# Two transformer blocks on one core: where the low halves of weights and norms are made, fp16 lookups in the routing, and four moves of small steps

## The chip, the core and the metric

One core of one Trainium2 chip runs the whole program in one launch. The metric is the device time of one execution in microseconds. TensorE is the matrix engine, VectorE (DVE) and ScalarE (ACT) the elementwise engines, GpSimd (POOL) the fourth, and SyncE (SP) issues most transfers.

## What is computed

The input is x, 256 tokens by 1024, in float32. The first block is modulated by a condition vector. It has two attentions (a sparse one with an index score and top 64 keys, and a "stick-breaking" one with cumulative products), and then a product-key mixture of experts: each token takes 16 of 128 sub-keys on two sides, 16 of their 256 sums, and so 16 of 16384 experts for each of 8 heads. The second block has a mixer (short convolution, block attention, gated linear attention), a cross attention on a memory of 256 tokens, and a convolutional ffn of width 2752. Cut to what the change touches, the routing of the experts is

```
s1, i1 = lax.top_k(s[:, :, 0], PEER_TOPK)
s2, i2 = lax.top_k(s[:, :, 1], PEER_TOPK)
cand = (s1[..., :, None] + s2[..., None, :]).reshape(t, PEER_HEADS, PEER_TOPK * PEER_TOPK)
cand_idx = (i1[..., :, None] * N_KEYS + i2[..., None, :]).reshape(t, PEER_HEADS, PEER_TOPK * PEER_TOPK)
top_s, pos = lax.top_k(cand, PEER_TOPK)
eidx = jnp.take_along_axis(cand_idx, pos, axis=-1)
```

## The kernel before

**Split products.** Every float32 product is made of three products of rounded halves: high by high, high by low, low by high. Weights stream in units of 128 x 1024. For each unit ScalarE casts the high half (`splits`, L1334, with the cast in L1343), and VectorE (`lows_until`, L1888, L1894) or POOL (`units`, L2696, L2702) subtracts it from the unit to get the low half. TensorE waits in `unit` for the low of a unit (semaphore `lo_v` or `lo_g`) and makes 24 matmuls with it, in the ffn and the projections 24 of 256 columns, in v 12 of 512 (all through the helper in L635). SyncE loads the next unit into a slot once the low of the slot's last unit is there.

**The order of work.** A plan (`stream_plan`) lists all units: w_ada, the projections of the first block up to w_o, then w_pq (16 units, queries of the routing), u (128), v (128), the w2 units, w_up (43) and w_dn (22). `lead_of` (L241) says how many units ahead of TensorE a high half is cast, `buffers` (L110 and below) gives from it, for each position i, the units whose cast (`hi_at[i]`) and whose low (`lo_at[i]`, one position later and never behind the unit) are made there. `on_pool` (L250) says which lows POOL makes: every second one in w_pq and in u before unit 56 (TB0), every third from u 120 to the ffn and in the ffn, with some left out, among them w2_o to w2_xo. Each engine runs its own program over the same list. Steps that are not weights (attention, routing, norms) are generators in `Jobs`; at each unit an engine takes one step of up to three of them, so that `yield` spaces them by units.

**Routing** (`route_steps`, L2264, on VectorE, one step a unit from w_pq on). Eight passes of three steps find the 16 best of 128 key scores (MAX8, FIND_INDEX8, MATCH_REPLACE8, L2281 to L2295); eight times three steps make and search the 256 candidates of a head (L2309 to L2326); then, for two halves of the tokens, some small operations (L2340 to L2351) and two lookups. A lookup turns 128 positions (8 heads x 16) into indices: it compares them with 0 to 15 (L2359, 2048 elements), multiplies with the 16 indices (L2362, 2048) and sums over the 16 (L2367). All in float32. TensorE transposes the results beside u 45 and u 52, and from u 54 on the gates are placed.

**Norms.** VectorE scales a tile (L1980), ScalarE rounds it to the high half, and POOL makes the low half (`norm_steps`, L2723, L2729) for norm 2 (the memory, beside v), norm 3 (in front of the mixer) and norm 5 (in front of the ffn). Norm 1, which has a shift, has its low on VectorE (L1984).

**Behind w_o.** The first two units of w_pq multiply the unscaled rows. VectorE then scales their results (L2254 to L2259) and ScalarE copies them out with a bias (L1635) when `q_r` says so; its cast of w_pq 4 comes after that.

**Stick masks.** POOL masks the diagonals of the stick attention (L2779, L2784) in two rounds of four heads, and adds the index mask to the position bias of eight heads (`masked`, L2766), six of them between the halves of the first round and behind it.

**Gated linear attention** (`gla_steps`: L1192 TensorE, L1763 ScalarE, L2516 VectorE, L2812 POOL). It starts behind w2_mv and the block attention; its first steps make the decays (L1770 to L1785: Abs, Exp, Ln, then the exponentials of their sums).

Of the kernel before, what the change touches and what calls it, by code (L numbers as in the profile page):

```python
# [210 lines left out]
def stream_plan():  # L211
# [29 lines left out]
    def lead_of(i):  # L241
        return 0 if i < QI0 - 1 else 4 if QA0 - 2 <= i < PA0 else 3 if i < PQ0 + 1 else 2 if i < XK0 - 2 else 3 if i < XL0 else 4 if i < XL0 + 2 else 5 if i < UP0 else 6
# [87 lines left out]
def scaled_before(q):  # L330

    return q - (q > 4)
# [38 lines left out]
def build(nc, A, out, scratch, x_kept):  # L371
    with ExitStack() as ctx:
# [98 lines left out]
        eq = PR[:, o96 + 6144:o96 + 8192]  # L471
        qh = [PR[:, 22528 + i * 512:22528 + (i + 1) * 512] for i in range(3)]
# [7 lines left out]
        tb = [z.bitcast(F16) for z in (flat(rT[:, 0:4, :]), xTf[:, 0:1024], xTf[:, 1024:2048])]  # L480
        t_row = [z[:, 0:512].rearrange("p (a i b) -> p a i b", a=2, b=2) for z in tb]
# [64 lines left out]
        mg_sum, mg_hi, mg_lo, pk_mm, pk_s = (sem(n) for n in ("mg_sum", "mg_hi", "mg_lo", "pk_mm", "pk_s"))  # L546
        rt_c, rt_d, rt_e, rt_f, rt_p, rt_m = (sem(n) for n in ("rt_c", "rt_d", "rt_e", "rt_f", "rt_p", "rt_m"))
# [81 lines left out]
        def tensor_program(t):  # L629
# [552 lines left out]
            lin("w2_mk", 4, hk, mh, both=True, alone=4)  # L1182
            one("w2_lr", hk, mh)
            lin_nat("w2_mv", hkt, mh, 512)

            def need_m():
                t.wait_ge(*evac("w2_mq", 1))
                t.wait_ge(*evac("w2_mk", 1))

            jobs.start(attend(ATT_M, need_m, lambda: t.wait_ge(*evac("w2_mv", 1))))  # L1190

            def gla_steps():  # L1192
# [3 lines left out]
                St = bmm[:, 2048:2816].rearrange("p (c e) -> p c e", c=3)  # L1196
                o = claim(6)
# [16 lines left out]
                yield  # L1214
                yield
                yield
# [42 lines left out]

            jobs.start(gla_steps())  # L1260
            lin("w2_gk", 2, hk, mh)
# [68 lines left out]
        def scalar_program(s):  # L1330
# [310 lines left out]

            def gate_weights(tt):
                s.wait_ge(rt_d, tt + 1)
                S.activation(g2[:, tt, :], g2[:, tt, :], ACT.Exp).then_inc(rt_e, 1)
# [115 lines left out]
            nat_copy("w2_mv", mv, 512)  # L1760
            jobs.start(attend(ATT_M, lambda: None))

            def gla_steps():  # L1763
# [4 lines left out]
                dec = sm[:, 120:124]  # L1768
                s.wait_ge(g_p, 1)
# [16 lines left out]
                yield  # L1786
                yield
                yield
# [22 lines left out]
            jobs.start(gla_steps())  # L1811
            lin_copy("w2_gk", 2, gqk)
# [71 lines left out]
        def vector_program(v):  # L1884
# [90 lines left out]
            def norm_steps(i, src, gain, shift=None):  # L1975
                for j in range(8 if shift is None else 10):
# [5 lines left out]
                    if shift is not None and j >= 2:  # L1982
                        v.wait_ge(n_hi, 8 * scaled_before(i) + j - 1)
                        V.scalar_tensor_tensor(out=H[:, 1, j - 2, :], in0=rT[:, ROW[(j - 2) % 4], :], scalar=shift(j - 2),  # L1984
# [268 lines left out]
            norm(1, xT, lambda j: sm[:, 24 + j:25 + j], shift=lambda j: mod[:, 24 + j:25 + j])  # L2253
            V.tensor_copy(rT[:, 1, :], recip(1)).then_inc(q_r, 1)  # L2254
# [9 lines left out]
            def route_steps():  # L2264
# [69 lines left out]
                e3, e4 = eq.rearrange("p (a i) -> p a i", i=16), eq.rearrange("p (h k i) -> p h k i", h=8, k=16)  # L2334
                io = iota[:, 0:16].rearrange("p (o i) -> p o i", o=1).broadcast_to((128, 128, 16))
# [683 lines left out]
```

## Time and profile before

| | |
|---|---|
| median of 3 runs | 1407.16 us (1403.23 to 1407.29) |
| the profiled execution's own time | 1406.49 us |
| its span, first to last instruction | 1404.8 us |
| mean granted clock of TensorE | 0.993 |
| busy: TensorE, VectorE, ScalarE, POOL | 97%, 77%, 60%, 25% |
| chain that ended last: TensorE, VectorE, ScalarE | 78%, 14%, 4% |

All durations below are of the one profiled execution. A row of the timeline gives the start from the first instruction of the span, the time to the end of the last instruction merged in it, engine, line, operation, what it writes and reads, and in brackets how long the engine was idle before it and whose work ended that. Matmuls are pipelined and their ends are modelled, so the spacing of starts is read rather than the busy share.

### The profile page before, as it was taken

How to read it: one execution, taken by the hardware profiler on the slowest of the kernel's cores; microseconds unless marked ns; L12 is line 12 of the kernel's file. 1: busy time of each engine (PE TensorE's matmuls, PEld its weight loads, DVE VectorE, ACT ScalarE, POOL GpSimd, SP SyncE). 2: the span in 40 equal slices, each digit the busy share in tenths (PEclk: the TensorE clock that was granted, in tenths of full speed). 3: DMA queues.
4: the chain of work that ended last, by engine and by line, in shares of the span. 5: the costliest groups of instructions: out<-in, count | busy, mean ns of one | idle time of the engine just before them, and what ended most of it. 6: DMA issues, size and time to landing. Idle time of an engine off the chain costs nothing.

```text
span 1404.8 us, 25319 instructions
## 1 busy us (share of the span) xinstructions
PE 1363.8 (97%) x10144; PEld 1265.8 (90%) x10144; DVE 1082.1 (77%) x1857; ACT 836.9 (60%) x1457; POOL 354.2 (25%) x223
## 2 busy tenths in 40 slices
PE   7999999999998999999999999999999999999997
PEld 5988989999998999999988888887888889899997
DVE  7789898668899888899576666677667577898862
ACT  3556776454553688787554444565556667777641
POOL 3216101234444000000222322343222221343200
PEclk9999999999999999999999999999999999999998
DMA  9859775556664555555566666666666536376630
GB/s 385 278 193 304 238 246 173 196 166 191 194 185 150 166 163 157 162 153 163 167 224 192 195 190 195 222 189 185 193 208 250 184 103 187 106 237 203 205 107 31
DMA packets 73719, 268.21 MB, mean 191 GB/s; under 512 B 8401, under 2 KB 9730, under 8 KB 72834
## 3 DMA queue, kind: packets, MB, share of 16 engines
q1 hardware_dynamic: 71280, 256.41, 57.9%
q10 hardware_dynamic: 1426, 7.56, 1.5%
q0 software_dynamic: 896, 2.62, 0.5%
q8 instruction: 81, 1.33, 0.4%
q14 instruction: 36, 0.29, 0.1%
HBM read 262.88 MB, written 3.67 MB: 190 GB/s over the span
## 4 chain that ended last, share of the span: by engine, by line
PE 78%; DVE 14%; ACT 4%; DMA 1%; issue 1%; POOL 0%; DVEq 0%; ACTq 0%; POOLq 0%
PE bank L635 78%; DVE split L1894 4%; DVE ada_acc L1929 2%; DVE PR L2362 1%; ACT split L1343 1%; DMA ringb<-in_w_ada 1%; DVE PR L2359 1%; DVE rT L1980 1%; DVE PR L2367 0%; PE bank L816 0%; DMA ringb<-in_w_g 0%; ACT PB L1460 0%; DVE H L2448 0%; DMA vecs<-in_vecs 0%; DVE MH L1996 0%
## 5 line engine op out<-in xcount | busy, mean ns | idle before, releaser
L635 PE MATMUL bank<-H,split 128*128 128x256 f32 x5832 | 704.6, 281 | 14.1 <-DVE split L1894 12.9
L635 PEld LDWEIGHTS bank<-H,split 128*128 128x128 f32 x5832 | 682.8, 189 | 20.6 <-DVE split L1894 15.9
L1343 ACT CAST split<-ringb 128x1024 fp32r<-128x1024 f32 x350 | 365.6, 1047 | 270.5 <-PE bank L635 254.7
L635 PE MATMUL bank<-split,H 128*128 128x512 f32 (+1 forms) x1728 | 390.1, 387 | 1.5 <-ACT PB L1362 1.4
L635 PEld LDWEIGHTS bank<-split,H 128*128 128x128 f32 x1728 | 320.4, 188 | 69.1 <-issue 1.8
L2702 POOL TENSOR_TENSOR split<-ringb,split 128x1024 fp32r<-128x1024 f32 x88 | 218.5, 2484 | 640.5 <-ACT split L1343 640.5
L1894 DVE TENSOR_TENSOR split<-ringb,split 128x1024 fp32r<-128x1024 f32 x262 | 332.1, 1271 | 58.9 <-ACT split L1343 58.8
L2448 DVE TENSOR_TENSOR H<-PR,H 128x256 fp32r<-128x256 f32 x128 | 135.1, 1056 | 105.5 <-ACT H L1697 105.4
L1894 DVE TENSOR_TENSOR split<-far,split 128x1024 fp32r<-128x1024 f32 x78 | 102.5, 1322 | 32.1 <-ACT split L1343 31.9
L1343 ACT CAST split<-far 128x1024 fp32r<-128x1024 f32 x89 | 92.7, 1048 | 53.0 <-PE bank L635 40.0
L2716 POOL TENSOR_TENSOR rT<-rT 128x256 f32<-128x256 f32 x25 | 28.9, 1156 | 174.5 <-ACT rT L1392 172.9
L1673 ACT ACTIVATE PR<-bank 128x512 f32<-128x512 f32 (+31 forms) x59 | 28.6, 485 | 61.8 <-PE bank L635 61.1
L635 PE MATMUL bank<-act_t,split 128*128 128x256 f32 x528 | 60.3, 276 | 0.1
L635 PEld LDWEIGHTS bank<-act_t,split 128*128 128x128 f32 x528 | 60.0, 188 | 0.3 <-DVE act_t L2671 0.3
L1655 ACT ACTIVATE xT<-cst,rT 128x128 f16<-128x128 f32 x168 | 55.2, 435 | 0.0
L2421 DVE SCALAR_TENSOR_TENSOR PR<-bank,PR 128x224 f32<-128x224 f32 (+31 forms) x64 | 33.3, 520 | 27.6 <-PE bank L635 27.1
L1697 ACT CAST H<-PR 128x256 fp32r<-128x256 f32 x128 | 51.1, 400 | 0.5 <-PE bank L635 0.5
L635 PE MATMUL bank<-Ym,split 128*128 128x256 f32 x336 | 41.5, 283 | 1.5 <-DVE Ym L2055 1.5
L635 PEld LDWEIGHTS bank<-Ym,split 128*128 128x128 f32 x336 | 40.2, 189 | 2.1 <-DVE split L1894 1.7
L2702 POOL TENSOR_TENSOR split<-far,split 128x1024 fp32r<-128x1024 f32 x11 | 28.2, 2562 | 53.9 <-ACT split L1343 53.9
L635 PE MATMUL bank<-PA 64*128 64x256 f32 (+4 forms) x176 | 25.9, 372 | 8.3 <-POOL PA L2739 8.3
L1929 DVE SCALAR_TENSOR_TENSOR ada_acc<-ringb,cond,ada_acc 128x1024 f32<-128x1024 f32 x24 | 32.2, 1343 | 1.5 <-DMA ringb<-in_w_ada 0.8
(307 smaller groups left out, 1266.2 us busy)
## 6 DMA issues: line engine op xcount, KB each, us to landing
ringb<-in_u SPq DMA_DIRECT2D x128, 512.0 KB, 3.9
ringb<-in_v SPq DMA_DIRECT2D x128, 512.0 KB, 4.5
ringb<-in_w_ada SPq DMA_DIRECT2D x28, 512.0 KB, 5.8
far<-in_w_up SPq DMA_DIRECT2D x26, 512.0 KB, 4.7
far<-in_w_ada SPq DMA_DIRECT2D x20, 512.0 KB, 5.3
ringb<-in_w_up SPq DMA_DIRECT2D x17, 512.0 KB, 4.7
ringb<-in_w_pq SPq DMA_DIRECT2D x16, 512.0 KB, 4.0
far<-in_w_dn SPq DMA_DIRECT2D x14, 512.0 KB, 3.8
```

The costliest lines, as they stand in the source:

```text
L635: return TE.matmul(o, l, r, start=start, stop=stop, skip_group_check=True)
L1343: S.copy(buf(m)[0], slots[P.slot[m]]).then_inc(hi_done, 1)
L1655: S.activation(z[:, i // 2, :, i % 2], iota, ACT.Abs, bias=cpn[:, 4 * g + i:4 * g + i + 1]).then_inc(t_abs, 1)
L1673: ins = S.activation(d[:, :, n:T], o[:, :, n:T], ACT.Gelu)
L1697: S.copy(cf[i % 8][0], P3[:, i, :]).then_inc(c_hi, 1)
L1894: V.tensor_tensor(lo, slots[P.slot[m]], hi.bitcast(F32), ALU.subtract).then_inc(lo_v, 1)
L1929: V.scalar_tensor_tensor(out=acc, in0=w, scalar=cond[:, k:k + 1], in1=acc, op0=ALU.mult, op1=ALU.add).then_inc(ada_done, 1)
L1980: V.scalar_tensor_tensor(out=rT[:, ROW[j % 4], :], in0=src[:, j, :], scalar=gain(j), in1=recip(i), op0=ALU.mult, op1=ALU.mult).then_inc(n_ ...
L2421: V.scalar_tensor_tensor(out=d[:, 0:n, :], in0=o[:, 0:n, :], scalar=DOWN16, in1=d[:, 0:n, :], op0=ALU.mult, op1=ALU.mult).then_inc(t_out, 1)
L2448: V.tensor_tensor(lo, P3[:, i, :], hi.bitcast(F32), ALU.subtract).then_inc(c_lo, 1)
L2702: G.tensor_tensor(lo, slots[P.slot[m]], hi.bitcast(F32), ALU.subtract).then_inc(lo_g, 1)
L2716: G.tensor_tensor(acc, acc if k > 1 else rT[:, square_row(q, 0), :], rT[:, square_row(q, k), :], ALU.add).then_inc(sq_add, 1)
```

## The change

1. `on_pool`: outside the ffn and the first two units of w_qi POOL makes no weight low any more; VectorE makes them. The lows of norms 2, 3 and 5 move to VectorE's `norm_steps`, one for each tile, two tiles behind the scaling. POOL's `norm_steps` goes.
2. The lookups run on fp16 in another order of axes: positions and indices are cast, compared with a table of 0 to 15 that ScalarE writes once (`io16`), multiplied, and summed by three additions that halve the length (2048, 1024, 512) and a last one that writes float32.
3. `lead_of` is 3 up to w_pq 2, so that ScalarE casts w_pq 4 in front of the copy of the first queries; VectorE calls `unit` and `lows_ahead` once in front of its copies, and later for five units instead of six.
4. POOL adds the index mask of heads 2 to 7 (twelve additions) in one piece behind the first round, instead of in two pieces.
5. The generator of the gated linear attention starts in front of w2_mv and of the attention; one `yield` comes first, and three yields behind the decays become six.

```
     def lead_of(i):
-        return 0 if i < QI0 - 1 else 4 if QA0 - 2 <= i < PA0 else 3 if i < PQ0 + 1 else 2 if i < XK0 - 2 else ...
+        return 0 if i < QI0 - 1 else 4 if QA0 - 2 <= i < PA0 else 3 if i < PQ0 + 3 else 2 if i < XK0 - 2 else ...
...
-        if XK0 - 1 <= i < XK0 + 7:
-            return False
-        return (PQ0 <= i < U0 + TB0 and i % 2 == 0) or (i >= U0 + TB0 + 64 and i % 3 == 0)
+        return i >= UP0 and i % 3 == 0
...
+            s.wait_ge(n_lo, 8 * scaled_before(1) + 8)
+            S.copy(io16.rearrange("p (i q) -> p i q", i=16), iota[:, 0:16]...broadcast_to((128, 16, 128))).then_inc(rt_i, 1)
...
             def norm_steps(i, src, gain, shift=None):
-                for j in range(8 if shift is None else 10):
+                both = MH if i == 2 else H
+                for j in range(10):
...
-                    if shift is not None and j >= 2:
+                    if j >= 2:
                         v.wait_ge(n_hi, 8 * scaled_before(i) + j - 1)
+                    if j >= 2 and shift is None:
+                        V.tensor_tensor(both[:, 1, j - 2, :], rT[:, ROW[(j - 2) % 4], :], both[:, 0, j - 2, :].bitcast(F32), ALU.subtract).then_inc(n_lo, 1)
...
+            unit("w_pq")
+            lows_ahead()
             V.tensor_copy(rT[:, 1, :], recip(1)).then_inc(q_r, 1)
...
+                v.wait_ge(rt_i, 1)
+                behind(0)
+                for tt in range(2):
+                    rc.up(V.tensor_copy(tf16[:, tt, :, :, :], tf[:, tt, :, :].rearrange("p (h c) i -> p c i h", c=2)))
...
-                        rc.up(V.tensor_tensor(e3, io, ps_, ALU.is_equal))
+                        rc.up(V.tensor_copy(pos16.rearrange("p (k h) -> p k h", k=16), pos))
+                        behind(0)
+                        rc.up(V.tensor_tensor(tri3(e16, 16), tri3(io16, 16), pos16...broadcast_to((128, 16, 128)), ALU.is_equal))
                         yield
                         behind(0)
-                        rc.up(V.tensor_tensor(e4, e4, tk, ALU.mult))
+                        rc.up(V.tensor_tensor(by(e16, 16), by(e16, 16), tk, ALU.mult))
                         yield
...
+                        for dst, src in ((e8, e16), (e4_, e8), (e2, e4_)):
+                            n = dst.shape[1]
+                            behind(0)
+                            rc.up(V.tensor_tensor(dst, src[:, 0:n], src[:, n:2 * n], ALU.add))
                         behind(0)
-                        V.tensor_reduce(cpf[:, tt, s2, :], e3, AX, ALU.add).then_inc(rt_f, 1)
+                        V.tensor_tensor(pos, e2[:, 0:128]..., e2[:, 128:256]..., ALU.add).then_inc(rt_f, 1)
...
-            units("w_pq", 6)
+            units("w_pq", 5)
...
-                if w == 0:
-                    masked(range(2, 5))
                 for i in range(4):
                     g.wait_ge(k_e2, 4 * w + i + 1)
                     G.tensor_tensor(diagonals(zs[i][1]), diagonals(zs[i][1]), up2, ALU.mult).then_inc(k_m2, 1)
                 if w == 0:
-                    masked(range(5, 8))
+                    masked(range(2, 8))
...
-            units(8)
-            jobs.start(norm_steps(2))
-            units(39)
+            units(8 + 39)
             jobs.finish()
             units(2 + 1)
+            g.wait_ge(c_lo, 128)
             G.memset(uv[:, :, 0:2], 0.0).then_inc(cv_z, 1)
...
-            norm(3)
...
-            norm(5)
```

On TensorE, ScalarE and VectorE alike the fifth item reads (TensorE's shown):

```
+            lin("w2_mk", 4, hk, mh, both=True, alone=4)
+            one("w2_lr", hk, mh)
             jobs.start(gla_steps())
+            lin_nat("w2_mv", hkt, mh, 512)
...
+            jobs.start(attend(ATT_M, need_m, lambda: t.wait_ge(*evac("w2_mv", 1))))
```

## Rows read from the trace of the kernel before

**Rows 1.** The page, busy time of each engine (share of the span) and instructions.

```profile
PE 1363.8 (97%) x10144; PEld 1265.8 (90%) x10144; DVE 1082.1 (77%) x1857; ACT 836.9 (60%) x1457; POOL 354.2 (25%) x223
```

**Rows 2.** Who TensorE waited for: us in total, times, longest us.

```profile
PE bank L635 <- DVE split L1894: 12.9, 9, 2.5
```

**Rows 3.** Busy us of each engine by stretch, granted clock, transfer share, GB/s.

```profile
319.14:335.46 16.32, 16.32 (x146) 16.32 (x146) 13.07 (x68) 7.75 (x9) 7.21 (x3) 1.00 0.66 195
351.78:368.10 16.32, 16.32 (x146) 16.32 (x146) 14.27 (x40) 7.76 (x9) 7.22 (x3) 1.00 0.67 196
...
413.18:461.87 48.69, 41.95 (x331) 41.15 (x330) 48.48 (x28) 20.52 (x24) 20.43 (x7) 0.93 0.49 149
```

**Rows 4.** Timeline of TensorE from 400 to 480: start, us, instructions merged.

```profile
423.24 13.23 PE L635 MATMUL bank<-H,split 128*128 128x256 f32 x96 [2.35 <-DVE split L1894]
...
436.55 11.55 PE L635 MATMUL bank<-H,split 128*128 128x256 f32 x96
450.30 5.71 PE L635 MATMUL bank<-H,split 128*128 128x256 f32 x48 [2.19 <-DVE split L1894]
458.14 4.62 PE L635 MATMUL bank<-H,split 128*128 128x256 f32 x24 [2.13 <-DVE split L1894]
...
462.85 11.14 PE L635 MATMUL bank<-H,split 128*128 128x256 f32 x96
```

**Rows 5.** Timeline of VectorE from 405 to 463.

```profile
415.50 4.38 DVE L2362 TENSOR_TENSOR PR<-PR 128x2048 f32<-128x2048 f32 x1
419.80 3.38 DVE L1894 TENSOR_TENSOR split<-ringb,split 128x1024 fp32r<-128x1024 f32 x1
```

**Rows 6.** Groups of VectorE instructions over the whole span: busy us, mean ns, idle.

```profile
L2309 DVE TENSOR_TENSOR PR<-PR 128x256 f32<-128x256 f32 x16 | 11.9, 784 | 0.1
...
L2359 DVE TENSOR_TENSOR PR<-cst,PR 128x2048 f32<-128x2048 f32 x4 | 9.2, 2288 | 0.1
L2665 DVE TENSOR_TENSOR ftmp<-ftmp 128x256 f32<-128x256 f32 x22 | 9.1, 415 | 0.0
```

**Rows 7.** Groups of VectorE from 500 to 650, where POOL does nothing.

```profile
L1894 DVE TENSOR_TENSOR split<-ringb,split 128x1024 fp32r<-128x1024 f32 x46 | 56.0, 1218 | 0.0
...
L2399 DVE TENSOR_TENSOR rt<-rt,cpw 128x512 f16<-128x512 f16 x45 | 18.7, 416 | 0.0
```

**Rows 8.** Timeline of POOL.

```profile
419.67 2.43 POOL L2702 TENSOR_TENSOR split<-ringb,split 128x1024 fp32r<-128x1024 f32 x1 [1.94 <-ACT split L1343]
```

**Rows 9.** Timeline around the fifth unit of w_pq, all engines, then TensorE alone.

```profile
258.71 0.51 ACT L1436 ACTIVATE H<-rT,mod 128x256 fp32r<-128x256 f32 x1 [0.28 <-DVE rT L1980]
...
261.16 0.84 ACT L1635 ACTIVATE PR<-bank,sm 128x256 f32<-128x256 f32 x2 [1.95 <-DVE bank L2259]
261.89 1.99 ACT L1343 CAST split<-ringb 128x1024 fp32r<-128x1024 f32 x2
...
264.25 4.58 PE L635 MATMUL bank<-H,split 128*128 128x256 f32 x24 [2.54 <-DVE split L1894]
```

**Rows 10.** Timeline of POOL and of TensorE around the norm of the memory.

```profile
936.01 2.38 POOL L2702 TENSOR_TENSOR split<-ringb,split 128x1024 fp32r<-128x1024 f32 x1 [4.88 <-ACT split L1343]
...
971.02 2.39 POOL L2702 TENSOR_TENSOR split<-ringb,split 128x1024 fp32r<-128x1024 f32 x1 [5.71 <-ACT split L1343]
...
937.35 1.46 PE L635 MATMUL bank<-rT,cst 128*128 128x256 f32 x6
```

**Rows 11.** Timeline of TensorE from 1076 to 1128.

```profile
1078.20 9.49 PE L635 MATMUL bank<-H,split 128*128 128x256 f32 x72
1089.00 5.73 PE L635 MATMUL bank<-H,split 128*128 128x256 f32 x48 [1.31 <-DVE split L1894]
...
1116.16 3.07 PE L635 MATMUL bank<-split,H 128*128 128x256 f32 x24 [1.36 <-ACT PB L1362]
...
1123.62 1.30 PE L635 MATMUL bank<-PB 64*128 64x128 f32 x16 [0.90 <-ACT PB L1472]
```

**Rows 12.** Timeline of TensorE in the stage of the stick attention.

```profile
128.90 1.46 PE L635 MATMUL bank<-zbuf,PA 128*64 128x256 f32 x8 [1.12 <-POOL zbuf L2784]
```

More of the change, by code:

```diff
@@ L241, in lead_of @@
     def lead_of(i):
[L242 removed]
+        return 0 if i < QI0 - 1 else 4 if QA0 - 2 <= i < PA0 else 3 if i < PQ0 + 3 else 2 if i < XK0 - 2 else 3 if i < XL0 else 4 if i < XL0 + 2 else 5 if i < UP0 else 6
     P.buffers(ring_of, lead_of, {QI0 + 2: QI0 + 1}, (7,))
@@ L471, in build @@
         eq = PR[:, o96 + 6144:o96 + 8192]
+        eq16 = eq.bitcast(F16)
+        e16, e8, e4_, e2, pos16 = (eq16[:, a:b] for a, b in ((0, 2048), (2048, 3072), (3072, 3584), (3584, 3840), (3840, 3968)))
+        tf16 = cand.bitcast(F16).rearrange("p (t c i h) -> p t c i h", t=2, c=2, i=16)
         qh = [PR[:, 22528 + i * 512:22528 + (i + 1) * 512] for i in range(3)]
@@ L1181, in tensor_program @@
             mh = normed(3)
[L1182 to L1190, printed above, removed]
             def gla_steps():
@@ L1213, in gla_steps @@
                 last.then_inc(g_p, 1)
-                yield
-                yield
-                yield
+                for _ in range(6):
+                    yield
                 t.wait_ge(g_v, GV["qk"])
@@ L1640, in scalar_program @@
                     jobs.start(key_scores(i))
+            s.wait_ge(n_lo, 8 * scaled_before(1) + 8)
+            S.copy(io16.rearrange("p (i q) -> p i q", i=16), iota[:, 0:16].rearrange("p (i q) -> p i q", q=1).broadcast_to((128, 16, 128))).then_inc(rt_i, 1)
             def gate_weights(tt):
@@ L1785, in gla_steps @@
                 S.activation(dec, bT[:, 63:256:64], ACT.Exp).then_inc(g_a, 1)
-                yield
-                yield
-                yield
+                for _ in range(6):
+                    yield
                 for i in range(2):
@@ L1811, in scalar_program @@
             jobs.start(gla_steps())
+            nat_copy("w2_mv", mv, 512)
+            jobs.start(attend(ATT_M, lambda: None))
             lin_copy("w2_gk", 2, gqk)
@@ L2512, in vector_program @@
             unit("w2_lr")
-            units("w2_mv", 4)
-            jobs.start(attend(ATT_M, lambda: v.wait_ge(bmm_in, 16)))
             def gla_steps():
@@ L2531, in gla_steps @@
                 V.tensor_scalar(la, la, 1.0 / 16.0, None, ALU.mult).then_inc(g_v, 1)
-                yield
-                yield
-                yield
+                for _ in range(6):
+                    yield
                 v.wait_ge(g_a, GA["dec"])
@@ L2576, in vector_program @@
             jobs.start(gla_steps())
+            units("w2_mv", 4)
+            jobs.start(attend(ATT_M, lambda: v.wait_ge(bmm_in, 16)))
             units("w2_gk", 2)
@@ L2721, in adds @@
                     pass
-            def norm_steps(i):
-                for j in range(8):
-                    tmp = rT[:, ROW[j % 4], :]
-                    both = MH if i == 2 else H
-                    hi, lo = both[:, 0, j, :].bitcast(F32), both[:, 1, j, :]
-                    g.wait_ge(n_hi, 8 * scaled_before(i) + j + 1)
-                    G.tensor_tensor(lo, tmp, hi, ALU.subtract).then_inc(n_lo, 1)
-                    yield
-            def norm(*a, **k):
-                for _ in norm_steps(*a, **k):
-                    pass
             g.wait_ge(rb_in, 16)
```

22 lines of the change are left out of this document (16 added, 6 removed).

## The prediction

> **What bounds the kernel.** I read the page first: TensorE is busy for 97% of the span [rows 1], so time can only come from its idle gaps, from matmuls that run slowly, or from less work. The change takes no matmul away. The view of who waited for whom gives TensorE 12.9 us behind the weight lows of VectorE, the largest wait after the start [rows 2]. The timeline of TensorE then says where. A unit of weights is 24 matmuls of 256 columns and takes 2.72 us when nothing is late: six units last 16.32 us, of which POOL makes three lows [rows 3]. In the lookups of the routing, behind 413 us, there are gaps of 2.35, 2.19 and 2.13 us, all ended by a low [rows 4]. Two of the batches behind them are also slow: 13.23 us for 96 matmuls against 11.14 for the same 96 at 462.85, and 4.62 us for 24, where 24 matmuls end after 2.99 (5.71 for 48, less 2.72). The granted clock of that stretch is 0.93 [rows 3]: part of it ran at 1.2 GHz instead of 2.4. With 0.4 us in the batch at 436.55 (11.55 against 11.14), the stretch loses 6.67+2.09+1.63+0.4 = 10.8 us.
>
> Why are those lows late? Three things must be seen together. The product of a lookup, 2.29 us when alone, took 4.38, and the low behind it 3.38 instead of 1.22 [rows 5 to 7]. At 419.80 that low began 0.13 us after POOL's own low of 2.43 us [rows 8], and took nearly the sum of the two. In the stretch 413.18 to 461.87 VectorE is busy 48.48 of 48.69 us [rows 3]. Its work there is four lookups of three operations on 2048 elements, 2.29 us each (27.5), seven lows (8.5) and some 1.6 us of small ones, 37.6 us in all. So about 11 us are VectorE standing behind POOL, since both read two SBUF tensors.
>
> The Trainium skill says the same in "GPSIMD Engine Reference", Key points: the SBUF interfaces are shared, and VectorE contends when it has two SBUF inputs. The trace agrees with its 3.38 us.
>
> **The change, part by part.** The sum is made against the profiled execution, 1406.49 us (span 1404.8); the median of the three runs is 0.67 higher.
>
> (a) Lookups. The 36 to 37 lows that POOL makes in w_pq and u before unit 56 go to VectorE, and each lookup becomes a chain of seven fp16 operations. A tensor_tensor of 512 fp16 took 416 ns, one of 256 fp32 415 ns, one of 2048 fp32 2288 ns [rows 6, 7]; so 148 ns plus 1.045 ns for each pair of halves. 2048 halves then take 1.22 us, 1024 0.68, 512 0.42, 256 0.28; the cast of positions and the last sum (128 elements of fp32) 0.28 each. A lookup is 0.28+1.22+1.22+0.68+0.42+0.28+0.28 = 4.38 us. Bounds: 4.38 from these rows, and 7.5 if every form makes one element per step only (0.28+2.29+2.29+1.22+0.68+0.42+0.28). I take 4.38, since the rows of 512 have a broadcast operand too. The stretch holds 14 units (331 matmuls), 38.1 us at full speed. VectorE needs 17.5 for lookups, 14 lows of 1.22 (17.1), 1.6 of small ones and up to 0.8 for the two copies of the index table: 37.0 us. It fits. I leave 0.5 us for a step that is late: the stretch gives back **10.3 us** (about 3 at the 7.5 bound).
>
> The Trainium skill, "VectorE: DVE Perf Modes", What auto-detection actually checks, wants every tensor in 16 bits with step one for the doubled rate; its table gives 1224 ns for 2048. By it comparison, product and the first three sums qualify, and the cast and the last sum do not.
>
> What pays for the lows elsewhere? In the search of the key scores six units show 13.07 us of VectorE work [rows 3]. Three more lows of 1.22 make 16.7 against 16.32: 0.4 us late in six units, 0.9 in the thirteen such units behind w_pq (in w_pq the key-score matmuls leave more room). In the candidate stage it is 14.27+3.66, less what its four sums at L2309 no longer lose to POOL (784 ns on average instead of 415, 1.5 in all [rows 6]), so 16.4: just what there is. A low is made a unit ahead: its cast can start two units (5.44 us) before TensorE needs it and takes 1.0 (two in 1.99 [rows 9]), the low 1.22, which leaves a reserve of 3 us. The cover is this reserve; if it is used up, each further unit costs 0.1 us. ScalarE's new copy of the position table (2048 elements, about 2 us by its casts of 1024) stands in front of one cast and eats 2 of the 3 us once. Cost: nothing.
>
> The same skill page, The DRAIN you can't avoid, lets no operation start before the pipe of the last is empty. By it lows take their full 1.22 us, as counted above; with the overlap that neighbouring starts show the stretch needs 1.1 us less.
>
> (b) Fifth unit. TensorE waits 2.54 us for the low of w_pq 4 and then needs 4.58 us for 24 matmuls instead of 2.99: 4.1 us. The cast stands on ScalarE behind two ACTIVATEs of 0.84 us, which wait 1.95 us for VectorE [rows 9]. With a lead of 3 it comes before that wait, when the norm's last activation ends at 259.2, and ends at 260.2. On VectorE the new call that would make the low stands before the copies only by its name: the plan puts low 4 at the position of w_pq 2, and unit and lows_ahead reach w_pq 1 alone. So the low follows the copies, which release ScalarE at 261.16, and ends near 262.4; TensorE was free 2.54 us before 264.25, at 261.7. 0.7 us remain, and without the long gap I expect no fall of the clock: **3.4 us**.
>
> (c) Norm of the memory. POOL's weight lows come every 8.16 us; from 936.01 to 971.02 the distance is 35.01 instead of 32.64, and six summing matmuls explain some 1.2 of the 2.37 between [rows 10]. **1.1 us** come from the loop scale, two casts, coefficient low, weight low, in which POOL holds VectorE up by 0.34 a unit. On VectorE the norm's low lies under the casts.
>
> (d) Norm 3. 72 matmuls from 1078.20 and the gap to 1089.00 take 10.80 us, 8.16 at full speed: 2.6 lost, 1.31 of it behind a low [rows 11]. Now VectorE waits for the cast at every tile (added wait: behind it are the weight lows, and TensorE behind these), and its lows 2 and 3 come after take_queries and a weight low: I work out 1.7 us of waits. **0.9 us** gained (0 to 2.3). Norm 5 is hidden by the unscaled units: nothing.
>
> (e) Decay steps. They issue no DMA; those that they need are issued before. Their three activations with table loads move from the attention to w2_mv, where ScalarE has one cast per unit and a lead of three units. The waits of 1.36 and 0.90 us for ScalarE's copies [rows 11] go: **2.25 us** (0 to 2.3). Next late would be the softmax chain.
>
> (f) Stick masks. The 1.12 us wait for POOL's mask [rows 12] ends with ScalarE's exponential, not with POOL's queue. What can be gained is VectorE's delay by six mask additions; they return later in one block of twelve. Between +1.5 and -1, I take **0.4 us**. The c_lo wait before the memset has only two sums behind it, and these wait for later work.
>
> Lows in u's end and in v (40) cost nothing: VectorE has room, and slots come free earlier. Sum: 10.3+3.4+1.1+0.9+2.25+0.4 = 18.4 us; 1406.5-18.4 = **1388.1 us**.
>
> **Rivals.** (1) VectorE is full. For: the search stage needs 16.7 of 16.32. Against: the lookups have room, and the reserve covers 0.1 us a unit for thirty units. If fp16 forms run at one element per step, VectorE needs 49.5 us where 38.1 and a reserve of 3 are there; and TensorE loses some 8 us again; 18.4-8 = 10.4 are left: 1396. Chance 0.14. (2) Slower: POOL is not what lengthens VectorE's instructions; transfers or ScalarE are, in the whole route stage. Then all 65 lows of the stage can take 2.2 us instead of 1.22 (64 us on top), and one in two of them 32; less 3 us of reserve and about 6 of room in w_pq some 23 are left, and the time is 1388+23 = 1411. It decides from 3.1 us of VectorE work per unit. Against: without POOL 46 lows average 1218 ns [rows 7]. 0.03. (3) The fifth unit's edit does not do what it says beyond the lead, and the clock still falls there: 1390 to 1392. 0.05. (4) More is freed than counted, in the stick stage and the mixer: 1383. 0.10. (5) The moves of (c) to (f) cancel and the lookups give half: 1403. 0.05. Forecast: 0.63.
>
> **Numbers.** A measurement of this kernel tells 0.3% (4.2 us) from no change. Cases 1, 3, 4 and the forecast are faster, 0.92; case 5 counts as same; case 2 as slower. The range 1382 to 1397 takes in all but 2 and 5.
>
> **What would show it.** Right: no gap over 1 us and a clock of 1.00 between 405 and 463 us, fp16 comparisons of 1.22 us, no VectorE low over 1.5 us before the ffn, a gap near 0.7 us in front of w_pq 4, none at w2_gk. Wrong: comparisons near 2.3 us, new gaps in the candidate stage, or lows of 2 us and more with POOL idle.

## The result: 1391.9 us after 1405.3, and the profile after

The changed kernel takes 1391.91 us, median of 11 runs (1387.92 to 1400.02); the kernel before takes 1405.30 beside it (1401.45 to 1411.5, 11 runs). The ratio is 0.9907, 95% interval 0.9891 to 0.9923. 13.4 us are gone where 18.4 were forecast. Every ratio leaves out runs at a clearly lower granted clock, such as one of 1689.55 us at 0.753 among the repeats of the changed kernel. The profiled execution took 1391.84 us (span 1390.0, 14.8 less than before).

Who TensorE waited for, after (us in total, times, longest):

```profile
PE bank L638 <- DVE split L1900: 3.8, 7, 0.8
...
PE bank L638 <- DVE H L1992: 1.5, 1, 1.5
...
PE bank L638 <- POOL zbuf L2792: 0.6, 1, 0.6
```

The 12.9 us of [rows 2] are 3.8, and the longest wait for a weight low is 0.8 instead of 2.5. New is L1992, the norm lows on VectorE. Busy time by stretch (us, then PE, PEld, DVE, ACT, POOL, granted clock, transfer share, GB/s):

```profile
409.10:452.10 43.00, 43.00 (x368) 43.00 (x367) 38.18 (x61) 22.42 (x26) 0.00 (x0) 1.00 0.59 185
318.67:335.62 16.95, 16.95 (x146) 16.95 (x145) 16.37 (x71) 7.75 (x9) 0.00 (x0) 1.00 0.60 194
```

Both stretches answer to [rows 3]. The one with the lookups has TensorE busy throughout and a clock of 1.00 where it was 0.93. But look at the second row: 146 matmuls, six units of weights, take 16.95 us instead of 16.32, with TensorE busy all the time, no wait, and a granted clock of 1.00. The groups of VectorE from 403 to 452 show the lookups (busy us, mean ns):

```profile
L1900 DVE TENSOR_TENSOR split<-ringb,split 128x1024 fp32r<-128x1024 f32 x18 | 22.0, 1221 | 4.6 <-ACT split L1346 4.3
L2378 DVE TENSOR_TENSOR PR<-rT,PR 128x2048 f16<-128x2048 f16 x4 | 4.9, 1226 | 0.1
L2381 DVE TENSOR_TENSOR PR<-PR 128x2048 f16<-128x2048 f16 x4 | 4.9, 1219 | 0.0
L2388 DVE TENSOR_TENSOR PR<-PR 128x1024 f16<-128x1024 f16 x4 | 2.7, 685 | 0.0
L2388 DVE TENSOR_TENSOR PR<-PR 128x512 f16<-128x512 f16 x4 | 1.7, 425 | 0.1
L2390 DVE TENSOR_TENSOR PR<-PR 128x128 f32<-128x128 f16 x4 | 1.6, 389 | 0.1
L2388 DVE TENSOR_TENSOR PR<-PR 128x256 f16<-128x256 f16 x4 | 1.2, 292 | 0.1
L2376 DVE CAST PR<-PR 128x128 f16<-128x128 f32 x4 | 1.1, 264 | 0.0
```

An fp16 comparison takes 1226 ns where the fp32 one took 2288 [rows 6], a low 1221 where one took 3.38 us [rows 5]. The timeline of TensorE, after:

```profile
261.18 3.00 PE L638 MATMUL bank<-H,split 128*128 128x256 f32 x24 [0.44 <-DVE split L1900]
...
304.44 127.45 PE L638 MATMUL bank<-H,split 128*128 128x256 f32 x1080
...
1068.51 13.60 PE L638 MATMUL bank<-H,split 128*128 128x256 f32 x114 [1.51 <-DVE H L1992]
...
1211.84 0.62 PE L638 MATMUL bank<-H,split 128*128 128x256 f32 x3 [0.51 <-DVE split L1900]
1212.97 12.30 PE L638 MATMUL bank<-H,split 128*128 128x256 f32 x106 [0.51 <-DVE split L1900]
```

The wait in front of w_pq 4 is 0.44 us instead of 2.54 [rows 9], and the granted clock stayed at 1.00 behind it. 1068.51 is norm 3, and 1211.84 and 1212.97 are two waits in front of the scaled units of w_up, where before had none. The waits of 1.36 and 0.90 us in the mixer [rows 11] are gone.

**Where the time went.** Both kernels issue the same 8856 matmuls on weights, so the start of the nth can be compared. By stretch, the distance between two such starts, before and after, in us:

| stretch | before | after | difference |
|---|---|---|---|
| to the first matmul, and up to the stick stage (600 matmuls) | 130.28 | 128.53 | -1.75 |
| fifth unit (1440 to 1488) | 11.54 | 7.98 | -3.56 |
| u, units 5 to 37 (1872 to 2664) | 89.76 | 93.28 | +3.52 |
| lookups, u from unit 38 (2664 to 3024) | 53.00 | 42.99 | -10.01 |
| norm of the memory (5860 to 6100) | 55.45 | 54.40 | -1.05 |
| norm 3, w2_mq and w2_mk (6480 to 6552) | 10.80 | 10.35 | -0.45 |
| mixer (6552 to 6888) | 65.99 | 63.13 | -2.86 |
| start of the scaled w_up (7380 to 7500) | 13.99 | 15.19 | +1.20 |
| all other stretches | | | +0.2 |

The third line is the surprise: 792 matmuls, no gap among them in either kernel, and 3.52 us more. Row 304.44 above holds them.

**Two paces.** In every trace of this study a matmul of 256 columns starts either 113.3 or 117.7 ns behind the last, for hundreds of matmuls on end, at a granted clock of 1.00. The group view of TensorE from 325 to 400 us shows it in the mean (busy us, mean ns), first before, then after:

```profile
L635 PE MATMUL bank<-H,split 128*128 128x256 f32 x665 | 75.5, 276 | 0.0
```

```profile
L638 PE MATMUL bank<-H,split 128*128 128x256 f32 x639 | 75.4, 281 | 0.0
```

665 against 639 matmuls in the same 75 us. Between two such weight matmuls that follow each other directly, I add up what the distance of their starts is over 113.3 ns. Where that is under 20 ns it is called slow pace here: 10.0 us in the trace of before and 14.4 in that of after. What is over 20 ns is called late starts, and matmuls at the low clock, each some 100 ns over, are in it too: it falls from 37.5 to 23.2 us. So the late starts fell by 14.3 us and the pace gave 4.4 us back; the rest of the 14.8 us between the spans lies at matmuls of 512 columns, at the other matmuls and in an earlier start.

### The profile page after: what moved, and what is told of

It is laid out like the page before. It is cut to its first block, busy times and chain, and to the rows that moved or that the text cites. A ratio compares the mean times of both kernels' runs of the same rounds, so it can differ in the third digit from the quotient of the medians.

```text
span 1390.0 us, 25338 instructions
## 1 busy us (share of the span) xinstructions
PE 1359.9 (98%) x10144; PEld 1264.8 (91%) x10144; DVE 1063.5 (77%) x1982; ACT 839.9 (60%) x1458; POOL 125.2 (9%) x116
## 4 chain that ended last, share of the span: by engine, by line
PE 85%; DVE 10%; ACT 2%; DMA 1%; issue 1%; POOL 0%; DVEq 0%; POOLq 0%; ACTq 0%
PE bank L638 84%; DVE split L1900 2%; DVE ada_acc L1935 2%; DMA ringb<-in_w_ada 1%; DVE rT L1987 1%; ACT split L1346 0%; PE bank L819 0%; DMA ringb<-in_w_g 0%; DMA vecs<-in_vecs 0%; DVE MH L2006 0%; DVE PA L2155 0%; DVE H L1992 0%; DVE PA L2143 0%; DVE sm L2153 0%; DVE H L1994 0%
## 5 line engine op out<-in xcount | busy, mean ns | idle before, releaser
L1900 DVE TENSOR_TENSOR split<-ringb,split 128x1024 fp32r<-128x1024 f32 x342 | 421.4, 1235 | 47.0 <-ACT split L1346 46.5
L2472 DVE TENSOR_TENSOR H<-PR,H 128x256 fp32r<-128x256 f32 x128 | 54.4, 426 | 137.2 <-ACT H L1703 137.2
L1900 DVE TENSOR_TENSOR split<-far,split 128x1024 fp32r<-128x1024 f32 x81 | 103.0, 1283 | 23.5 <-ACT split L1346 23.2
L2435 DVE TENSOR_TENSOR xT<-rt,cpw 128x512 f16<-128x512 f16 x84 | 31.7, 419 | 0.0
L638 PEld LDWEIGHTS bank<-PA 64*128 64x128 f32 (+2 forms) x176 | 16.5, 181 | 15.0 <-issue 12.6
```

The costliest lines, as they stand in the source:

```text
L638: return TE.matmul(o, l, r, start=start, stop=stop, skip_group_check=True)
L1900: V.tensor_tensor(lo, slots[P.slot[m]], hi.bitcast(F32), ALU.subtract).then_inc(lo_v, 1)
L2435: ins = V.tensor_tensor(t_gate[g % 3][:, z, :, :, :], t_col[g % 2], of_four(gp[:, 2 + z, :], g), ALU.mult)
L2472: V.tensor_tensor(lo, P3[:, i, :], hi.bitcast(F32), ALU.subtract).then_inc(c_lo, 1)
```

## The experiments

**Once more.** The changed kernel unchanged.

> The changed kernel once more, unchanged. In its first trace 24 matmuls of 256 columns take either 2.72 us (113.3 ns each) or 2.83 us (117.7 ns each) with nothing late and a granted clock of 1.00; between 229 and 452 us the slow pace holds nearly throughout, which the kernel before shows at other places. Theory A: the pace is set by the order of instructions ahead of a stretch, so this run has the slow pace in the same places and its median lies within 2 us of 1391.9. Rival B: the pace is drawn anew in each execution; then the trace shows it elsewhere, and the sum of matmul time over the fast pace (15.0 us in the first trace, 10.6 in the kernel before) differs by some us.

Median of 7 runs 1393.78 us. The stretch of 792 matmuls takes 93.28 us again and the lookups 42.98: the pace in u comes back the same, and 14.2 us of slow pace stand against 14.4. At other places it differs, as B has it: the first 144 matmuls run at 117.7 where the first trace had 113.3.

**One matmul more.** In the key scores of head 7:

```
+                for _ in range(1 if c == 7 else 0):
+                    last = mm(o[:, 384:512], z[:, T + 128:2 * T], skt[:, (2 * c + 1) * 128:(2 * c + 2) * 128], True, True)
```

> The changed kernel, in which the last matmul of the last group of key scores (head 7, fp32, 128 x 128) is made twice with the same result. In the first trace each group of these turned the pace of the 256-column matmuls behind it from one value to the other. Theory A: one matmul more in the group turns the pace for the whole of u up to the routing transposes: 113.3 instead of 117.7 ns for some 1190 matmuls, 5.2 us less, so about 1387. Rival B (the pace hangs on something else, on transfers or on VectorE, which is fuller than before): it stays at 117.7, and the time is that of the changed kernel plus 0.2 us.

1387.93 us (7 runs; ratio to before 0.9901, 0.9874 to 0.9929; single runs 1387.2 to 1389.5 and two above 1395). The timeline of TensorE at the last key scores, before (the row behind them, too), after (the row behind them is 304.44), and with the repeated matmul:

```profile
308.30 1.05 PE L635 MATMUL bank<-PR 128*128 128x128 f32 x8
309.11 111.79 PE L635 MATMUL bank<-H,split 128*128 128x256 f32 x984
```

```profile
303.64 1.05 PE L638 MATMUL bank<-PR 128*128 128x128 f32 x8
```

```profile
304.40 1.27 PE L638 MATMUL bank<-PR 128*128 128x128 f32 x10
305.43 122.67 PE L638 MATMUL bank<-H,split 128*128 128x256 f32 x1080
```

The 984 matmuls of before take 111.79 us, 113.6 ns each; the 1080 up to the first transposes take 127.45 in the changed kernel and 122.67 with the repeated matmul. The stretch of 792 takes 89.76, as before, and the lookups 42.13 instead of 42.99: 4.4 us of the 5.2 expected. The medians' distance to the changed kernel, 4.0 us, is the size expected, but the intervals of the two ratios overlap and two of the seven runs were no faster; the cause rests on the trace. VectorE is full there and still not the bound; the window of six units in this kernel:

```profile
322.10:338.40 16.30, 16.30 (x147) 16.30 (x146) 16.29 (x71) 7.77 (x9) 0.00 (x0) 1.00 0.63 196
```

VectorE is busy 16.29 of 16.30 us, and no matmul is late. So the slow pace isn't VectorE's doing.

**Half of part (a) each.** On the kernel before, the change's lines for the lookups alone (its point 2), and its weight lows alone:

```
-        return (PQ0 <= i < U0 + TB0 and i % 2 == 0) or (i >= U0 + TB0 + 64 and i % 3 == 0)
+        return i >= UP0 and i % 3 == 0
```

> The kernel before with the fp16 lookups alone; POOL keeps its weight lows. Theory A (VectorE is short of time in the lookups; operation length and POOL's lows both cost): the four lookups take 17.5 instead of 27.5 us alone, seven lows 8.5 and small ones 1.6, with some 8 us of standing behind POOL about 36 of 38.1 us: the 11.1 us of late starts in the lookups fall to 1 to 3, and the time to about 1396. Rival B (POOL's lows are the whole of it): gaps of about 2 us stay, 5 us or more are lost there, 1400 or above.

> The kernel before with POOL's weight lows outside the ffn moved to VectorE, lookups in float32. Theory A: in the lookups VectorE needs 27.5 us for lookups, 17.1 for fourteen lows and 1.6 for small ones, 46.2 us, where TensorE has 38.1 and a reserve of 3: 5 us of gaps and some 3 of slow clock stay of 11.1, so about 1402. No VectorE low is longer than 1.5 us outside the ffn. Rival B (POOL's lows are the whole of it): the 11.1 us go without the lookups' edit, 1394.

1404.22 us (10 runs; 0.9997, 0.9976 to 1.0019) and 1402.37 us (10 runs; 0.9987, 0.9966 to 1.0007): by the medians neither does anything, where 1396 and 1402 were expected. The traces say otherwise. Late starts in the lookups fall from 11.1 to 1.7 us and to 2.6 us. They leave out waits in front of the transposes there. By the whole stretch, less its slow pace, 52.4 us become 45.1 and 44.9, where the changed kernel has 41.4: of 11.0 us the lookups alone give 7.4 and the lows alone 7.5. The timeline of TensorE with the lookups alone, then with the lows alone:

```profile
434.66 0.30 PE L1044 MATMUL bank<-cst,PR 128*128 128x128 f32 x1 [1.18 <-DVE PR L2386]
...
435.62 20.93 PE L640 MATMUL bank<-H,split 128*128 128x256 f32 x168 [0.44 <-DVE split L1902]
```

```profile
445.62 3.00 PE L633 MATMUL bank<-H,split 128*128 128x256 f32 x24 [0.34 <-DVE split L1892]
...
459.41 3.80 PE L633 MATMUL bank<-H,split 128*128 128x256 f32 x31 [0.46 <-DVE split L1892]
```

The 8 us that I left for the second were 2.6, or 3.5 by the whole stretch: its waits are 0.3 to 0.5 us long, and behind them a unit takes 3.00 us at most, so no stretch there ran at the low clock. That is nearer to rival B, and its median near the expected 1402 is a hit for a wrong reason. In the first, the timelines of VectorE and then of POOL show that fp16 operations stand behind POOL too:

```profile
414.85 1.23 DVE L2374 TENSOR_TENSOR PR<-rT,PR 128x2048 f16<-128x2048 f16 x1
416.12 3.32 DVE L2377 TENSOR_TENSOR PR<-PR 128x2048 f16<-128x2048 f16 x1
```

```profile
414.92 3.43 POOL L2722 TENSOR_TENSOR split<-ringb,split 128x1024 fp32r<-128x1024 f32 x1 [3.26 <-ACT split L1348]
```

The comparison began 0.07 us before POOL's low and takes its own 1.23 us; the product behind it takes 3.32 instead of 1.22 and ends 1.1 us after POOL's low. This is the contention that the Trainium skill describes in "GPSIMD Engine Reference", Key points, and the trace agrees for 16 bits as well. What ate the gain in both traces is the pace: u ran at 93.28 us in both, and the ffn, which takes 154.0 us in the traces of before and after from the start of matmul 7500 of the 8856 to that of the last, took 157.7 and 159.7. In all the slow pace is 17.9 and 20.6 us there, against 10.0 before. The trace of the weight lows is of a run of 1407.67 us, 5.3 above its median, so what the pace took from that median is argued from one trace. Timeline of TensorE at the scaled w_up, before and with the lookups alone:

```profile
1227.11 103.12 PE L635 MATMUL bank<-H,split 128*128 128x256 f32 x905
```

```profile
1221.20 109.00 PE L640 MATMUL bank<-H,split 128*128 128x256 f32 x921
```

905 matmuls in 103.12 us, 921 in 109.00.

**The pace taken out.** The lookups alone and the repeated matmul.

> The kernel before with the fp16 lookups and the repeated key-score matmul. With the fp16 lookups alone the late starts in the lookups fell from 11.1 to 1.7 us, yet the median did not move, and u ran at 117.7 ns. Theory A (the slow pace in u ate 3.5 us of the gain, and in the ffn up to 6 more): u runs at 113.3, 89.8 instead of 93.3 us, and the median falls from 1404.2 to about 1400.5, with single runs between 1396 and 1405 by the pace of the ffn. Rival B: u stays at 93.3 us, or the time does not follow.

1398.31 us (10 runs; 0.9956, 0.994 to 0.9971), two single runs above 1403. u takes 89.76 us, the ffn 154.0. Late starts in the lookups are 2.8 us. The gain of the fp16 lookups shows once the pace behind it is the same: the median is 6.9 us lower, and the stretch of the lookups less its slow pace is 7.5 us shorter.

**The repeated matmul on the kernel before.**

> The kernel before with the one repeated key-score matmul of the last run but one, and nothing else. Theory A (the order of instructions ahead of a stretch sets the pace): in the kernel before u ran at 113.3 ns per 256-column matmul up to the lookups, so the repeated matmul turns it to 117.7: the 792 matmuls from the start of u to the lookups take 93.3 us instead of 89.8, and the kernel is 3.5 us slower by that stretch, about 1408. Rival B (the pace is set by how full VectorE is, which the repeated matmul only happened to relieve): 89.8 us and no difference, 1405.

1405.05 us (10 runs; 1.0003, 0.9987 to 1.0019), u 89.76 us. These are rival B's numbers: the pace does not turn, it stays fast, and theory A failed here. Rival B's cause, how full VectorE is, does not stand either. It was busy for 16.29 of 16.30 us above, and the pace was fast; with the fp16 lookups alone VectorE has no more to do in u than before, and the pace was slow (93.28 us). "One more turns it" is wrong as I had it; what stands is that behind ten records of key scores (five matmuls) u was fast in all five traces of this study, once behind the slow pace and four times behind the fast, and that eight turned whatever was ahead.

**What a group does to the pace.** Groups of repeated fp32 matmuls of 128 x 128, each of which makes two records, in front of blocks of u and w_up:

```
                             claim(b)
+                            for _ in range(GROUPS.get((name, p), 0)):
+                                mm(banks[b][:, 0:128], ident, ident, True, True)
```

> The changed kernel with groups of repeated fp32 matmuls of 128 x 128 in front of 19 blocks of u (four groups each of one, two, three; three of four; two of five and of six) and of 15 blocks of w_up (one to eight, then one to seven); they write where the block then starts anew, so the result stays. Theory A (the size of a group and the pace ahead of it decide the pace behind it): each size turns or keeps the pace in the same way each time it stands behind the same pace, so that its rows form a table without contradictions. Rival B (the pace behind a disturbance is drawn anew): equal sizes behind equal paces give both paces. The time itself says nothing: the added matmuls take some 20 us.

One run, 1416.94 us. The timeline of TensorE behind the first group of four matmuls (eight records); 48 matmuls last 5.70 us at the fast pace and 5.90 at the slow one:

```profile
378.84 5.90 PE L638 MATMUL bank<-H,split 128*128 128x256 f32 x48
384.57 1.06 PE L638 MATMUL bank<-cst 128*128 128x128 f32 x8
385.39 5.70 PE L638 MATMUL bank<-H,split 128*128 128x256 f32 x48
390.93 1.05 PE L638 MATMUL bank<-cst 128*128 128x128 f32 x8
391.74 5.90 PE L638 MATMUL bank<-H,split 128*128 128x256 f32 x48
397.47 1.28 PE L638 MATMUL bank<-cst 128*128 128x128 f32 x10
398.51 5.90 PE L638 MATMUL bank<-H,split 128*128 128x256 f32 x48
...
411.02 1.50 PE L638 MATMUL bank<-cst 128*128 128x128 f32 x12
412.28 5.70 PE L638 MATMUL bank<-H,split 128*128 128x256 f32 x48
```

An even number of matmuls (2, 4, 6, 8) turned the pace in all 16 groups; an odd number (1, 3, 5, 7) kept it in 17 of 18, the one exception being the first single one, which stood behind the slow pace and was followed by the fast. The kernels' own key scores are groups of four such matmuls, and behind all 79 of these that stand alone, in the 14 traces of this study, the pace turned. So behind these groups the pace is decided, not drawn, and that is why it comes back in u. The repeated matmul on the kernel before (five behind the slow pace, then the fast one) is a second exception.

The number alone does not decide it, though. In the first block two fp32 transposes of 128 x 128 (four records) once stand behind the fast pace and leave it fast, and four (eight records) stand behind the slow pace and leave it slow, in each of the 14 traces. The timeline of TensorE in the changed kernel shows the second case; both rows of 24 matmuls run at 117.7 ns:

```profile
196.46 3.10 PE L638 MATMUL bank<-Yb,split 128*128 128x256 f32 x24
199.40 1.03 PE L819 MATMUL bank<-cst,PA 128*128 128x128 f32 x8
200.19 3.07 PE L638 MATMUL bank<-Yb,split 128*128 128x256 f32 x24
```

And behind the groups of eight fp16 matmuls that place the gates the pace turned at some places and was kept at others, in each trace. Why the engine keeps or turns it no run shows.

**Norms 3 and 5 back on POOL.**

```
-                for j in range(10):
+                pool = i in (3, 5)
+                for j in range(8 if pool else 10):
```

and POOL's loop of the kernel before, called for 3 and 5.

> The changed kernel, with the norm lows of norms 3 and 5 back on POOL and those of norm 2 left on VectorE. Theory A (the moved norm lows are what TensorE waits for at w_up, 0.51 and 0.51 us, and at w2_mk, 1.51 us): the stall at w_up goes (1.2 us) and that at w2_mk falls to that of the kernel before with POOL's weight lows moved (0.7 us less), together 1.9 us: 1390 to 1391.5 with the slow pace in u. Rival B (POOL's subtractions hold VectorE up there, as the change supposes): no gain, and at w2_mk a loss of up to 0.5 us.

The timeline of TensorE at both places:

```profile
1068.07 12.17 PE L638 MATMUL bank<-H,split 128*128 128x256 f32 x105 [0.70 <-POOL H L2751]
...
1209.47 15.74 PE L638 MATMUL bank<-H,split 128*128 128x256 f32 x134
```

w2_mq and w2_mk take 9.13 instead of 10.35 us, and w_up 13.99 instead of 15.19, as before: 2.4 us in all, and the trace's time was 1390.88. At w2_mq and w2_mk part of this depends on the execution: the kernel before takes 10.80 us there, and with nothing but the repeated key-score matmul, far ahead of it, 8.91. But the median is 1397.44 (5 runs; 0.9948, 0.9931 to 0.9964): the four other runs took 1396.9 to 1397.8, where 1390 to 1391.5 were expected. In this trace the ffn's stretch has 2.1 us of slow pace. That the four others had more of it is what their times suggest; there is no trace of them.

**Decay steps and masks undone.**

> The changed kernel without two of its parts: decay steps back behind w2_mv, and the index mask of POOL in two pieces again. Theory A: the stretch from w2_lr's unit to the end of the mixer's attentions is 2.9 us longer (66.0 instead of 63.1), with waits of 1.36 and 0.90 us for ScalarE's copies; in the stick stage the wait for POOL's mask is 1.1 instead of 0.6 us: 3.4 us slower in all, where the pace of the matmuls is the same. Rival B (the mixer's waits went because VectorE no longer stands behind POOL, not because the steps moved): the stretch stays near 63.5 us.

The timeline of TensorE:

```profile
129.17 1.46 PE L638 MATMUL bank<-zbuf,PA 128*64 128x256 f32 x8 [1.13 <-POOL zbuf L2794]
...
1104.99 3.07 PE L638 MATMUL bank<-split,H 128*128 128x256 f32 x24 [1.36 <-ACT PB L1365]
...
1112.37 1.30 PE L638 MATMUL bank<-PB 64*128 64x128 f32 x16 [0.91 <-ACT PB L1475]
```

All three waits are back, at the sizes of [rows 11, 12]; the mixer takes 65.89 instead of 63.13 us. 1397.61 us (5 runs; 0.9953, 0.9937 to 0.9968), 5.7 us over the changed kernel's median where 3.4 were expected; the first 600 matmuls have 1.4 us of slow pace more in this trace. The mixer's waits are the steps', not POOL's.

**The lead undone.**

```
-... 3 if i < PQ0 + 3 else 2 ...
+... 3 if i < PQ0 + 1 else 2 ...
```

> The changed kernel with a lead of 2 for w_pq 3 and 4 again, and the new call of VectorE ahead of its copies kept. Theory A (the gain at the fifth unit is the lead's alone, the call does nothing): TensorE waits 2.5 us there again and the clock falls, 4.4 us of stall instead of 0.7: 3.6 us slower. Rival B (the call frees half of it): 2 us or less of stall.

The timeline of TensorE:

```profile
262.99 4.46 PE L638 MATMUL bank<-H,split 128*128 128x256 f32 x24 [2.54 <-DVE split L1900]
```

2.54 us of wait and 4.46 us for 24 matmuls, 11.42 us for the stretch instead of 7.98: the gain is the lead's, and the new call, which is in this kernel, does nothing. The one time is 1394.49.

How large the gain is depends on the clock. Without the lead the clock fell to 1.2 GHz behind this wait here, in the kernel before and with the weight lows alone (11.42, 11.54 and 11.46 us for the stretch). With the lookups alone, with the lookups and the repeated matmul, and with the repeated matmul alone it stayed at 2.4 GHz (9.95, 9.96 and 10.05 us), behind a wait just as long. The timeline of TensorE with the lookups alone:

```profile
262.77 3.00 PE L640 MATMUL bank<-H,split 128*128 128x256 f32 x24 [2.53 <-DVE split L1902]
```

So the lead gives back 3.5 us where the clock falls and 2.0 where it does not.

**Three edits together.** The repeated matmul, norm 3 on POOL, and in VectorE's new call

```
-            lows_ahead()
+            lows_until(st["pos"] + 2)
```

> The changed kernel with three edits: the repeated key-score matmul; the norm lows of norm 3 on POOL again (norm 5 stays on VectorE, since its two waits of 0.8 us at w_up are followed by the fast pace in all traces); and VectorE makes the low of w_pq 4 in front of its two copies instead of behind them. Theory A: 3.5 us from the pace in u, 1.2 from norm 3 (10.35 to 9.13 us for 72 matmuls), 0.7 from the wait at w_pq 4: 1391.9-5.4 = 1386.5. Rival B (a changed wait lets the ffn fall into the slow pace, as with both norms on POOL): up to 6 us more, 1390 to 1393.

1393.66 us (6 runs, 1386.5 to 1396.7; 0.9905, 0.9882 to 0.9929). All engines around 260 us, then TensorE:

```profile
260.59 1.23 DVE L1902 TENSOR_TENSOR split<-ringb,split 128x1024 fp32r<-128x1024 f32 x1 [0.37 <-ACT split L1348]
...
263.11 0.84 ACT L1640 ACTIVATE PR<-bank,sm 128x256 f32<-128x256 f32 x2 [2.56 <-DVE bank L2274]
```

```profile
264.10 4.59 PE L638 MATMUL bank<-H,split 128*128 128x256 f32 x24 [2.03 <-ACT PR L1640]
```

The low of w_pq 4 now waits for its cast, the copies wait for the low, ScalarE's activations start 3.9 us behind the first matmul of the stretch (263.11 less 259.2) instead of 2.2 (259.96 less 257.75), and TensorE waits 2.03 us for them. The stretch of the fifth unit takes 11.04 us instead of 7.98, which is 3.1 of the 7.2 us between the time and the 1386.5 expected; the ffn's slow pace (156.0 us instead of 154.0) is 2.0 more. The place behind the copies is the better one.

**Two edits.** Without the last.

> The changed kernel with two edits: the repeated key-score matmul and the norm lows of norm 3 on POOL; the low of w_pq 4 stays behind the copies. Theory A: u at 113.3 ns per matmul (89.8 us for 792 matmuls instead of 93.3), 9.1 to 9.4 us for the 72 matmuls of w2_mq and w2_mk instead of 10.35, so 3.5 and 1.0 us less than the changed kernel: about 1387.4 where the ffn keeps the fast pace, up to 6 us more in executions where it does not; a median of 1387 to 1390. Rival B: the edit at norm 3 brings the ffn into the slow pace more often (4 of 5 executions with both norms on POOL were above 1396): a median of 1392 or more.

1386.47 us (6 runs, 1385.6 to 1387.4 and one of 1393.1; ratio to before 0.9873, 0.9841 to 0.9904). u takes 89.76 us, w2_mq and w2_mk 9.58. w2_mq and w2_mk were expected at 9.1 to 9.4, and the median at 1387 to 1390. This is faster than before, and its median is 5.4 us below the changed kernel's; but the two weren't timed in one comparison, and the intervals of their ratios to before overlap (0.9891 to 0.9923 for the changed kernel).

## Why the forecast was right, and where it missed

The forecast case came about, within its range and in the main by its mechanisms; 3.8 us short of its sum. The sizes below are of one trace each, and single runs of either kernel lie 10 us or more apart. Step by step:

- **(a) Lookups**, 10.3 forecast: late starts fell by 11.0 us, and no VectorE low of the route stage is over 1.5 us (eight elsewhere ahead of the ffn still are, 1.67 to 1.77 us, where I had forecast none). The seven fp16 operations take 0.26, 1.23, 1.22, 0.69, 0.43, 0.29 and 0.39 us, 4.5 for a lookup where 4.38 were forecast. "VectorE: DVE Perf Modes", The perf-mode tier table, in the Trainium skill gives 1224 ns for 2048 elements of 16 bits, and the trace agrees (1226). The last sum, which writes fp32, takes 389 ns for 128 elements; that is more than the 0.28 us of one element per step, and why no run shows. That VectorE at 16.7 of 16.32 us in the search stage costs nothing also held: it is full there, and nothing is late. Not seen was how far either half would do alone: the lookups give 7.4 of the 11.0 us and the lows 7.5.
- **(b) Fifth unit**, 3.4: 3.56, 0.72 of late starts stay as worked out, and without the lead it comes back. That it agrees is in part luck: some 1.5 us of it are the low clock of the one trace that it was worked out from, and three of six traces without the lead do not have it.
- **(c) Norm of the memory**, 1.1: 1.05. With POOL's weight lows moved and the norm's lows still on POOL the stretch takes 55.39 us, against 55.45 before and 54.40 after, so the gain is the norm lows' own.
- **(d) Norm 3**, 0.9: 0.45. The wait is where I put it, 1.51 us for the norm's lows behind a weight low on VectorE. The stretch takes 9.64 us with the weight lows moved alone, so moving the norm's lows gave 0.7 of that back, and the 8.91 us above say that the 10.80 which I started from was not fixed either.
- **(d), its last sentence: "Norm 5 is hidden by the unscaled units: nothing."** This failed: 1.2 us lost against the trace of before (0.8 to 1.5 against the five traces that have the norm as before: 13.70 to 14.44 us). Eight norm lows of 0.42 us now stand on VectorE ahead of three weight lows, the first of which starts at 1210.56, when TensorE is about to be through with the unscaled units; TensorE waits twice. With the lows on POOL both waits go. The timeline of VectorE, after:

```profile
1209.56 1.09 DVE L1992 TENSOR_TENSOR H<-rT,H 128x256 fp32r<-128x256 f32 x3
1210.56 3.49 DVE L1900 TENSOR_TENSOR split<-far,split 128x1024 fp32r<-128x1024 f32 x3
```

- **(e) Decay steps**, 2.25: 2.86. **(f) Stick masks**, 0.4: 0.5 (the wait is 0.61 instead of 1.12 us). The rest of the 1.75 us in the table's first line is an earlier start (0.6) and pace (0.7), neither of which is the change's: the first weight matmul starts at 35.8 to 37.1 us in the 14 traces, and in the repeat of the changed kernel at 37.06.
- **The sum.** Without the pace the parts give 11.0+3.6+1.05+0.45+2.9+0.5-1.2 = 18.3 us, the forecast 18.4. That they agree is luck in part: what the lookups, the fifth unit, the decay steps and the masks gave beyond their terms (1.65 us) cancels what the norms fell short (1.7). The working took 24 matmuls at 2.72 us as the price of a unit "when nothing is late". That step failed: a unit costs 2.72 or 2.83 us, and the change turned u from the one to the other. It is 4.4 us net in the traces, of which 3.52 are u; 18.3 less 4.4, and the 0.6 of the start, are 14.5 of the 14.8 us between the spans.

Rival 1 (fp16 at one element per step) is excluded by 1226 ns; rival 2 (POOL isn't the cause) by the weight lows moved alone, which left 3.5 of 11.0 us, with no low of the route stage over 1.5 us. Rival 3's 1390 to 1392 is the measured time, yet not its mechanism: the clock did not fall. Rival 4 had its direction right in the mixer and the stick stage (3.4 us freed where 2.65 were counted), but this is far from 1383, and rival 5's lookups gave all of their term, not half.

## What to carry to other kernels

When every wait that was aimed at is gone and the time doesn't follow, compare the start of the nth matmul in both traces and read the distance from one matmul's start to the next in stretches without gaps; a difference of 4% there is as large as a whole edit. Test a part together with a check of the pace behind it, or a part that is worth 7 us can look like nothing in the median. Where two edits relieve the same engine, price the second on what the first leaves.

## What the hardware showed that was not expected

- At a granted clock of 1.00, 256-column matmuls with one weight load each run at 113.3 or 117.7 ns; either lasts over 1000 matmuls (1080 in 122.67 or 127.45 us). The cause in the engine stays open.
- An even number of fp32 matmuls of 128 x 128 between them turned the pace in the probe (16 of 16) and in the key scores (79 of 79), an odd number mostly kept it (17 of 18); transposes of the same size and number did not follow this. Behind waits of TensorE it came out either way: the ffn, whose code is the same in most of these kernels, took 154.0, 156.0, 157.7 or 159.7 us.
- Behind the same wait of 2.5 us for the low of w_pq 4 the clock fell to 1.2 GHz in some traces and stayed at 2.4 in others, which is 1.5 us for one stretch.
- fp16 with two SBUF inputs is held up by a tensor_tensor of POOL like fp32: 3.32 us instead of 1.22. One that had begun 0.07 us before POOL's was not held up (1.23); POOL's took 3.43 instead of 2.43.
